# Even mixer: rotations at the end of the first attention, a second attention three units deep

## The reference

```
ml_l = _mlstm_out(hl, pl[2], ml_g, dt)          # head norm * gain * sigmoid(gate)
lam = _diff_lambda(da_lam, lam_init)            # exp(sum lp0*lp1) - exp(sum lp2*lp3) + lam_init
ql = _apply_rope(ql, cos, sin)                  # latent tokens only
kl = _apply_rope(kl, cos, sin)

def _diff_attend(q, k, v, lam):
    s = jnp.einsum('bqhmd,bkhmd->bhmqk', q, k).astype(jnp.float32) * (DA_DQK ** -0.5)
    p = jax.nn.softmax(s, axis=-1)
    p = p[:, :, 0] - lam * p[:, :, 1]
    return jnp.einsum('bhqk,bkhv->bqhv', p.astype(v.dtype), v)

yl = jnp.concatenate([ml_l, _da_out(da_l, da_g, lam_init, dt)], axis=-1) @ w_out
```

## Time and profile before

| | |
|---|---|
| time, median of 3 runs | 4531.56 us (4529.86 to 4535.65) |
| the profiled execution's own time | 4527.05 us |
| its span, first to last instruction | 4525.2 us |
| PE busy | 4089.2 us, 90% |
| DVE busy | 3006.6 us, 66% |
| ACT busy | 2109.4 us, 47% |
| POOL busy | 400.4 us, 9% |
| granted TensorE clock, mean | 0.953 of 2.4 GHz |
| from the last matmul of stage 1 to the first of stage 7 | 1492.2 to 1614.53 us |

### The profile page before, as it was taken

The page is one execution under the profiler, slowest core; times in us unless marked ns, Lnnn a source line. Parts: engine busy times, 40 slices in busy tenths (PEclk is TensorE's granted clock), DMA queues, the critical chain, the costliest instruction groups (busy, mean ns, idle before and its releaser), DMA issues. The chain is left out here.

```text
span 4525.2 us, 71134 instructions
## 1 busy us (share of the span) xinstructions
PE 4089.2 (90%) x25056; PEld 3587.8 (79%) x25056; DVE 3006.6 (66%) x5888; ACT 2109.4 (47%) x3241; POOL 400.4 (9%) x470
## 2 busy tenths in 40 slices
PE   6997999959989677999999979999999769999998
PEld 5985889848977466888888868888888568888887
DVE  4555555555537649777777797777776688777776
ACT  4442444444434324555555545555554445555554
POOL 0000000000011015200000251000001044000000
PEclk9997999979989788999999989999999989999999
DMA  5554555554521031355555514555554121555554
GB/s 194 186 197 185 212 209 186 197 190 178 179 93 57 13 114 57 125 191 190 191 190 197 184 38 154 189 192 188 193 210 145 44 93 69 191 189 191 190 190 167
DMA packets 105284, 718.10 MB, mean 159 GB/s; under 512 B 13857, under 2 KB 14465, under 8 KB 21281
## 3 DMA queue, kind: packets, MB, share of 16 engines
q1 hardware_dynamic: 94688, 661.45, 40.8%
q0 software_dynamic: 8880, 52.12, 3.0%
q10 hardware_dynamic: 1552, 2.36, 0.2%
HBM read 709.48 MB, written 6.39 MB: 158 GB/s over the span
## 5 line engine op out<-in xcount | busy, mean ns | idle before, releaser
L228 DVE TENSOR_TENSOR units<-ring,units 128x1024 fp32r<-128x1024 f32 x1146 | 1390.5, 1224 | 535.9 <-ACT units L221 535.2
L221 ACT ACTIVATE units<-ring 128x1024 fp32r<-128x1024 f32 x1206 | 1272.8, 1056 | 959.3 <-PE ps L251 926.2
L3120 PE MATMUL ps<-wide,units 128*128 128x512 f32 x3072 | 759.0, 389 | 3.0 <-PEq L3018 3.0
L3120 PEld LDWEIGHTS ps<-wide,units 128*128 128x128 f32 x3072 | 576.3, 188 | 123.0 <-issue 3.5
L249 PE MATMUL ps<-units,weighted 128*128 128x512 f32 x1536 | 603.7, 393 | 8.7 <-DVE units L228 8.7
L250 PE MATMUL ps<-units,weighted 128*128 128x512 f32 x1536 | 603.0, 393 | 0.0
L251 PE MATMUL ps<-units,weighted 128*128 128x512 f32 x1536 | 598.2, 389 | 0.0
L3172 ACT ACTIVATE low_halves<-ps 128x256 f32<-128x256 f32 x384 | 147.7, 385 | 687.5 <-PE ps L3122 687.5
L3122 PEld LDWEIGHTS ps<-wide,units 128*128 128x128 f32 x3072 | 419.1, 190 | 29.9
L3122 PE MATMUL ps<-wide,units 128*128 128x256 f32 x3072 | 428.3, 282 | 0.0
L3190 DVE TENSOR_TENSOR gelued<-low_halves,ps 128x256 f32<-128x256 f32 x384 | 161.9, 421 | 377.6 <-ACT low_halves L3172 377.6
(11 more groups left out here) (497 smaller groups left out, 6504.3 us busy)
## 6 DMA issues: line engine op xcount, KB each, us to landing
ring<-in_stream SPq DMA_DIRECT2D x603, 1024.0 KB, 4.8
quad_ring<-in_mod_w POOLq DMA_DIRECT2D x12, 4096.0 KB, 14.1
front<-residuals_dram SPq DMA_DIRECT2D x5, 1024.0 KB, 7.0
gain_rows<-in_norm_gains SPq DMA_DIRECT2D x6, 512.0 KB, 4.5
peer_keys<-in_keys SPq DMA_DIRECT2D x3, 1024.0 KB, 5.1
ml_mask<-in_ml_mask SPq DMA_DIRECT2D x1, 2048.0 KB, 7.7
residuals_dram<-residual SPq DMA_DIRECT2D x2, 1024.0 KB, 6.7
front<-mod_rows_dram SPq DMA_DIRECT2D x4, 512.0 KB, 8.0
```

The source lines that it names most:

```text
L221: act.activation(K.parts(n)[0], K.raw(n), ACT.Copy).then_inc(K.sig("hi_made").sem, 1)
L228: dve.tensor_tensor(lo, K.raw(n), hi.bitcast(FP32), ALU.subtract).then_inc(K.sig("unit_split").sem, 1)
L3120: pe.matmul(both, hi[:, k, :], pair[:, :, k, :], start=(k == 0), stop=False)
```

## The change

What it does, stage by stage:

- Lambda is made inside stage 1: the parameters are loaded at its start, DVE works at steps 2 and 5 of the loop, ACT at step 3.
- The rotations move to the end of stage 1, on DVE, behind the head statistics. The mLSTM's gain is multiplied into the gate by one instruction, and 16 instructions of 128x128 (one for each tile and head) replace the three passes for each tile.
- Stage 3 becomes `turned_heads`: it also turns the mLSTM half of `even_mix` (4 more groups, ahead of q and k) and makes `both_pair` of it straight from PSUM. The scale of the scores goes into q.
- Stage 4 is rewritten: three units deep, one maximum instruction for both maps, one instruction that combines the maps in place, weights without the division; the division comes with the copy of the output. In the lists the maximum of unit u stands ahead of the combining of unit u-1. ACT also squares and sums each output.
- Stages 5 and 6 become the tail of the same block: one root for all 16 sums, 16 instructions of 128x128, 16 transposes, and `both_pair` straight from PSUM.

```diff
+                    if step == 2:
+                        dve.wait_ge(*lam_loaded.at(16))
+                        for n in range(2):
+                            last = dve.tensor_tensor(lp[:, 2 * n, :], lp[:, 2 * n, :], lp[:, 2 * n + 1, :], ALU.mult)
+                        order(dve, last)
+                        for n in range(2):
+                            last = dve.reduce_sum(lam[:, n:n + 1], lp[:, 2 * n, :], AX)
+                        last.then_inc(lam_summed.sem, 1)
+                    if step == 5:
+                        dve.wait_ge(*lam_exped.at(1))
+                        order(dve, dve.tensor_tensor(lam[:, 2:3], lam[:, 1:2], lam[:, 0:1], ALU.subtract))
+                        order(dve, dve.tensor_scalar(lam[:, 2:3], lam[:, 2:3], -LAM_INIT, None, ALU.add))
...
-                dve.wait_ge(*root_done.at(1))
+                tmp = seen[:, :, :, :].rearrange("p i m n -> p (i m) n")
+                dve.wait_ge(*rows_taken.at(4))
+                rotate(K, dve, rows[:, MT:TILES, 0:512].rearrange("p t (h d) -> p t h d", d=64), 32, sin, cos, tmp)
                 dve.wait_ge(*row_loaded.at(16))
                 dve.wait_ge(*gated.at(1))
-                g = row[:, :].rearrange("p (h d) -> p h d", h=ML_HEADS)
+                order(dve, dve.tensor_tensor(gate, gate, row[:, :].unsqueeze(1).broadcast_to([P, TILES, width]), ALU.mult))
+                dve.wait_ge(*rows_taken.at(8))
+                rotate(K, dve, rows[:, MT:TILES, 512:1024].rearrange("p t (h d) -> p t h d", d=64), 32, sin, cos, tmp)
+                dve.wait_ge(*root_done.at(1))
+                order(dve, dve.reciprocal(root, root))
                 for t in range(TILES):
-                    var = K.stat[:, 32 + 7 * t:32 + 7 * t + ML_HEADS]
-                    order(dve, dve.reciprocal(var, var))
-                    order(dve, dve.tensor_tensor(h[:, t, :, :], h[:, t, :, :],
-                                                 var.unsqueeze(2).broadcast_to([P, ML_HEADS, DV]), ALU.mult))
-                    order(dve, dve.tensor_tensor(h[:, t, :, :], h[:, t, :, :], g, ALU.mult))
-                    order(dve, dve.tensor_tensor(mix[:, t, 0:width].rearrange("p (h d) -> p h d", h=ML_HEADS), h[:, t, :, :],
-                                                 gate[:, t, :].rearrange("p (h d) -> p h d", h=ML_HEADS), ALU.mult))
+                    for n in range(ML_HEADS):
+                        d = slice(n * DV, (n + 1) * DV)
+                        last = dve.scalar_tensor_tensor(mix[:, t, d], h[:, t, n, :], root[:, t, n:n + 1], gate[:, t, d],
+                                                        ALU.mult, ALU.mult)
+                order(dve, last)
...
+                    if step == 3:
+                        act.wait_ge(*lam_summed.at(1))
+                        act.activation(lam[:, 0:2], lam[:, 0:2], ACT.Exp).then_inc(lam_exped.sem, 1)
...
+    sources = [[mix[:, t, c * P:(c + 1) * P] for t in range(TILES)] for c in range(4)]
+    for at in (0, 512):
+        sources += [[rows[:, t, at + h * P:at + (h + 1) * P] for t in range(TILES)] for h in range(4)]
...
+            for n in by_vector:
+                dve.wait_ge(*turned.at(n + 1))
+                if n < 4:
+                    dve.wait_ge(*rounded.at(n + 1))
+                    last = dve.tensor_tensor(pair[:, 1, n, :], bank(n), pair[:, 0, n, :].bitcast(FP32), ALU.subtract)
+                elif n < 8:
+                    last = dve.tensor_scalar(q[:, n - 4, :], bank(n), MEM_DH ** -0.5, None, ALU.mult)
+                else:
+                    last = dve.tensor_copy(k[:, n - 8, :], bank(n))
+                last.then_inc(taken[0].sem, 1)
...
+    DEEP = 3
...
+                for step in range(len(work) + 3):
+                    i = step
+                    if i < len(work):
+                        h, t = work[i]
+                        if i >= 2:
+                            pe.wait_ge(*exped.at(i - 1))
+                        for m in range(2):
+                            r = slice(m * 64, (m + 1) * 64)
+                            last = pe.matmul(scores(i)[:, m, :], q[r, h, t * P:(t + 1) * P], k[r, h, 0:keys(i)], start=True, stop=True)
+                        last.then_inc(scored.sem, 1)
+                    i = step - 2
+                    if 0 <= i < len(work):
+                        pe.wait_ge(*shared.at(i + 1))
+                        if i >= 2:
+                            pe.wait_ge(*copied.at(i - 1))
+                        for b in range(keys(i) // P):
+                            last = pe.transpose(K.ps[:, 4 + i % 2, b * P:(b + 1) * P], exps[:, i % DEEP, 0, b * P:(b + 1) * P],
+                                                K.ident[:, :])
+                        last.then_inc(turned.sem, 1)
+                    i = step - 3
+                    if i >= 0:
+                        h, t = work[i]
+                        pe.wait_ge(*copied.at(i + 1))
+                        if i >= 2:
+                            pe.wait_ge(*taken.at(i - 1))
+                        blocks = keys(i) // P
+                        for b in range(blocks):
+                            last = pe.matmul(result(i), flipped[:, i % 2, b * P:(b + 1) * P],
+                                             rows[:, b, 1024 + h * DV:1024 + (h + 1) * DV], start=(b == 0), stop=(b == blocks - 1))
+                        last.then_inc(made.sem, 1)
+                for h in range(heads):
+                    pe.wait_ge(*weighed.at(h + 1))
+                    for t in range(TILES):
+                        last = pe.transpose(K.ps[:, h, t * P:(t + 1) * P], out[:, h, t, :], K.ident[:, :])
+                    last.then_inc(columns.sem, 1)
...
+                for step in range(len(work) + 5):
+                    i = step
+                    if i < len(work):
+                        dve.wait_ge(*scored.at(i + 1))
+                        dve.tensor_reduce(bias[:, i, :], scores(i), AX, ALU.max, negate=True).then_inc(raised.sem, 1)
+                    i = step - 1
+                    if 0 <= i < len(work):
+                        dve.wait_ge(*exped.at(i + 1))
+                        order(dve, dve.reciprocal(share[:, i, :], sums[:, i, 1:2]))
+                        order(dve, dve.scalar_tensor_tensor(share[:, i, :], sums[:, i, 0:1], lam, share[:, i, :], ALU.mult, ALU.mult))
+                        n = keys(i)
+                        dve.scalar_tensor_tensor(exps[:, i % DEEP, 0, 0:n], exps[:, i % DEEP, 1, 0:n], share[:, i, :],
+                                                 exps[:, i % DEEP, 0, 0:n], ALU.mult, ALU.add).then_inc(shared.sem, 1)
+                        dve.reciprocal(sums[:, i, 0:1], sums[:, i, 0:1])
+                    i = step - 4
+                    if 0 <= i < len(work):
+                        h, t = work[i]
+                        dve.wait_ge(*made.at(i + 1))
+                        dve.tensor_scalar(out[:, h, t, :], result(i), sums[:, i, 0:1], None, ALU.mult).then_inc(taken.sem, 1)
+                dve.wait_ge(*squared.at(len(work)))
+                weight = 1.0 - LAM_INIT
+                dve.tensor_scalar(square, square, weight ** -2 / DV, weight ** -2 * EPS, ALU.mult, ALU.add).then_inc(mean_done.sem, 1)
+                dve.wait_ge(*root_done.at(1))
+                order(dve, dve.reciprocal(square, square))
+                dve.wait_ge(*row_loaded.at(16))
+                for h in range(heads):
+                    for t in range(TILES):
+                        last = dve.scalar_tensor_tensor(out[:, h, t, :], out[:, h, t, :], square[:, 4 * h + t, :],
+                                                        row[:, h * DV:(h + 1) * DV], ALU.mult, ALU.mult)
+                    last.then_inc(weighed.sem, 1)
+                for h in range(heads):
+                    dve.wait_ge(*rounded.at(h + 1))
+                    last = dve.tensor_tensor(pair[:, 1, 4 + h, :], K.ps[:, h, :], pair[:, 0, 4 + h, :].bitcast(FP32), ALU.subtract)
...
+                for step in range(len(work) + 6):
+                    i = step
+                    if i < len(work):
+                        act.wait_ge(*raised.at(i + 1))
+                        if i >= DEEP:
+                            act.wait_ge(*turned.at(i - DEEP + 1))
+                        n = keys(i)
+                        for m in range(2):
+                            last = act.activation(exps[:, i % DEEP, m, 0:n], scores(i)[:, m, :], ACT.Exp, bias=bias[:, i, m:m + 1],
+                                                  accum_out=sums[:, i, m:m + 1])
+                        last.then_inc(exped.sem, 1)
+                    i = step - 2
+                    if 0 <= i < len(work):
+                        act.wait_ge(*turned.at(i + 1))
+                        if i >= 2:
+                            act.wait_ge(*made.at(i - 1))
+                        n = keys(i)
+                        act.activation(flipped[:, i % 2, 0:n], K.ps[:, 4 + i % 2, 0:n], ACT.Copy).then_inc(copied.sem, 1)
```

(50 more changed lines are left out.)

177 lines of the change are left out of this document (51 added, 126 removed).

## The result

The changed kernel takes **4478.4 us** (median of 4 runs, 4476.28 to 4479.98) where the kernel before took 4533.6 (median of 4, 4529.86 to 4540.05): a ratio of **0.9882**, 95% interval 0.9867 to 0.9896. It is 55 us or 1.2% faster; 4484 was forecast, in a range of 4471 to 4503. The profiled execution took 4476.28 us, with a span of 4474.5 against 4525.2.

A forecast was written before the change was run, and what follows sets the result against it. Latency bounds the second attention: DVE and ACT wait for each other each unit. Savings 6.0 + 42.3 - 0.5 = 47.8 from the profiled 4527.05 give 4479; that run was 4.5 under the median, so 4484, range 4471 to 4503.

The forecast's parts named there:

- Stage 1: End of the first attention: with rotations and norm added, DVE's last instruction ends near 1501.0, 5.3 us later than before.
- POOL does not hold the rotations: Rival at the first attention's end: DVE never stands still for POOL's splits, ending at 1493.3 for 1501.0; 4476 us, chance 0.10.
- Turning: Transposing q, k and half the mixer's output, 12 groups: 9.0 us from DVE's last instruction to first scores, for 20.3.
- The loop: Second attention: DVE bounds it once the next maximum precedes the combining; 41 us taken, bounds 37.6 and 55.
- the two-unit chain: Second attention: exponentials, copy, values' product, scores and maximum take 5.2 us for two units of 2.75 at 512 keys.
- The sum by DVE's instructions (37.6): Second attention: DVE's work per unit, 2.75 us for 512 keys and 1.95 for 256, 8 of each.
- the filling: Second attention: start-up time included in the 41 us taken, where DVE's instructions alone sum to 37.6.
- PE bounds the second attention at 1.2 GHz: Rival: at the low clock PE's work makes that stretch 55 us for 41, and the whole 4498; chance 0.12.
- The depth gives nothing: Rival: some wait ties the second attention's engines to one unit again; 57 us for 41, whole 4500; chance 0.06.
- The tail: Last output to projection: square 0.4, open table load 1.3, mean to reciprocal 0.6, products 4.3, low parts 2.9, block end 0.6.
- The drain: End of the second attention: from the last combining to the last output 5.1 us, as before.
- slower than before: Rival behind the projection: PE's granted clock falls under 0.953, its 2688 us grow 1.8% and eat all 47.8; chance 0.02.

The follow-up runs named there:

- the kernel with the better parts together: The changed kernel with PE's next scores ahead of the values' product, the last weight split on DVE, and a spare root before the last two squares: 4475.09 us, ratio 0.9871.

## Why the prediction was right, point by point

**What bounded the kernel.** Right: the kernel before was bound there by waits, and the gaps on PE are where the time came from.

**The time.** It fits better than its parts, and that is luck. Against the 4479.2 that the sum gives for a profiled execution, 4476.3 was measured. The changed parts gave 5.3 more than forecast, the stretch ahead of them 2.9, and the stretch behind them, which the prediction took as a fixed length, took 5.3 back.

**Stage 1.** Right in kind, sized 1.2 too high. POOL does hold DVE's instructions of two SBUF tensors (rows of 2.52, 2.65 and 2.45 for 0.42), and "POOL does not hold the rotations" fell. The prediction let DVE stand still over both of POOL's adjoining splits. Instead DVE got one instruction in between them: the first long row ends at 1479.92, POOL's pair only at 1482.21. This is the case that the prediction named by the Trainium skill, "SBUF — State Buffer", section "SBUF: two separate sides"; the traces agree for DVE. For POOL they point the same way: the pair took 5.17 us here, and 4.78 at 1462.0, where DVE was idle. The prediction put 2.4 us on this case, which was too much: an instruction that slips in saves no more than its own 0.4. The three long rows stand still for 2.1 + 2.2 + 2.0 = 6.4 us together, for the 7.6 (4.8 and 2.8) of the prediction; that is the 1.2.

**Turning.** Right: 9.5 for 9.0.

**The loop.** The size was nearly right (38.1 to the start of the last combining for 41), the reason was half right. The step that failed is "Now DVE's list has the next maximum ahead of the combining, so ACT has its input while DVE combines", taken as sufficient, with the two-unit chain only as a remark beside it. The runs show that this order alone costs 31 us, and pays only when PE's list turns two units behind the scores. The distance deserved a term of its own. The sum by DVE's instructions (37.6) came near nevertheless, since the changed kernel has both, and since two errors offset each other: four units take 8.8 us of work (1522.99 to 1532.44, less 0.67 of waiting) for the 9.4 put, and DVE waits 5.0 us in the loop where 3.4 was put for the filling.

**"PE bounds the second attention at 1.2 GHz".** It did not: the clock was 0.96 for 0.78, and PE's busy share 86% for 62%. The Trainium skill, "TensorE: Matmul & The Clock Gate", section "A second HAM failure mode: psum-queue depth-cycling", had spoken for this rival; here the levels swung in the sparse loop, not in the dense one. Read in pieces of 2.5 us, the loop before goes down to 0.50 five times, the changed one once, to 0.60, near its start. Where the lists tied the engines together, the clock was 0.57.

**"The depth gives nothing".** It fell by the time (41 for 57), yet its wording mixed two things: the third exponentials buffer indeed gives nothing, the lists' distance a great deal.

**The tail.** Right: 2.3 from the last output to the norm's first product, with the table load open as said (1549.22, 1.28 us); 6.8 for products and low parts, where 7.2 was put. The drain from the last combining to the last output took 3.7 for 5.1, since PE ran at full clock there; with the old tail, at a clock of 0.50, it took 5.0 in the same loop. The table load (ACT) and the norm, root and lows (DVE) in rows:

```profile
1549.22 1.28 ACT L2643 ACT_TABLE_LOAD   x1
...
1550.78 0.26 DVE L2605 RECIPROCAL small<-small 128x16 f32<-128x16 f32 x1 [1.36 <-ACT small L2643]
1551.08 4.29 DVE L2609 SCALAR_TENSOR_TENSOR da_out<-da_out,small,row 128x128 f32<-128x128 f32 x16
1555.28 2.61 DVE L2614 TENSOR_TENSOR both_pair<-ps,both_pair 128x512 fp32r<-128x512 f32 x4
```

**Sum.** 53.1 us from the changed parts for the 47.8 forecast. The mis-sized terms are the loop (41 for 38.1), the drain (5.1 for 3.7) and stage 1's end (5.3 for 4.1), 5.5 together, against smaller ones the other way. The clock behind the projection stayed at 0.97, so "slower than before" had no ground; the 5.3 us that are lost there are not explained by it. What moving lambda by itself is worth was not tested.

## What to carry to other kernels

Before a step is moved ahead in one engine's list, follow what each other engine has queued behind the step that it passes: the same reordering was worth 17 us in the changed kernel, with PE's list two units behind, and cost 31 in the kernel before, with it one unit behind. How far the lists stand apart counts, not how many buffers there are; a count of buffers is tested by taking one away. When a chain is broken up, add up the next engine's instructions from start to start: that sum (37.6) came within 4 us of the loop here (38.1 to the last combining, 41.4 to the last output), in part because two errors offset each other. And compare what lies ahead of the change and behind it too: here it moved the time by 2.9 and 5.3 us.

## What the runs showed of the hardware beyond that

- POOL's split and DVE's instruction of two SBUF tensors take turns one by one, even when POOL has two in a row: 2.52 and 2.65 us for 0.42 over POOL's pair of 5.17. With the last split moved off POOL, the row in its place took 0.42 again.
- Over the same 208 matmuls the mean granted clock was 0.57 where F→O took 100.2 us, 0.69 (82.6), 0.78 (69.5), 0.77 (58.6), 0.87 (50.8), 0.89 (48.0), 0.96 (41.4) and 1.00 (40.4 and 38.0). On the whole it is higher where PE is fed more densely, but not in every case: 58.6 us have no higher clock than 69.5, and the kernel with the better parts together had 0.91 in 39.6 us. So a wait that is taken out can shorten the matmuls too; how much of each difference is the clock's was not separated.
- A loop in which PE works at low clock near the start is 1.0 to 1.6 us longer than the same one at full clock (41.4 against 40.4, and 39.6 against 38.0).
